# Another order in the HGRN ring, behind it, and at the start of the output stage, of a hybrid decoder layer on one core

## The reference

```python
h = rms_norm(x, norm_g)
aq, ak, av, ag, hq, hf, hi, hg = split(h @ w_in)     # eight groups of 512 columns
o_a = diff_attention(rope(norm(aq)), rope(norm(ak)), av)            # 4 heads, causal
hq = silu(hq);  f = lb + (1 - lb) * sigmoid(hf);  logf = log(f);  hk = 1 - f
# HGRN, 4 heads of 128, in chunks along the tokens, state S (128 x 128 of each head):
b   = cumsum(logf)
att[t, s] = sum_d hq[t, d] * hk[s, d] * exp(b[t, d] - b[s, d])      # s <= t
o_h = att @ hi + (hq * exp(b)) @ S
S   = exp(b_end) * S + (hk * exp(b_end - b)).T @ hi
mix = concat(rms_norm(o_a) * silu(ag), rms_norm(o_h) * silu(hg))
y   = x + mix @ w_out
```

## Time and profile before

| | |
|---|---|
| median of 3 runs | 1703.94 us (1701.72 to 1711.8) |
| the profiled execution | 1702.97 us |
| its span in the trace | 1700.8 us |
| mean granted TensorE clock | 0.975 of full speed |
| PE busy | 1563.5 us (92%) |
| DVE busy | 992.0 us (58%) |
| ACT busy | 774.9 us (46%) |
| POOL busy | 494.2 us (29%) |
| HBM traffic | 100 GB/s over the span |

### The profile page before, as it was taken

One profiled execution on the slowest core, in us unless ns is written; L12 is line 12 of the kernel. 1 busy time (PEld: TensorE's weight loads), 2 busy tenths in 40 slices (PEclk: granted clock), 3 DMA queues, 4 the chain that ended last, 5 costly groups with the idle time before them and its releaser, 6 DMA issues. The chain is left out here.

```text
span 1700.8 us, 24978 instructions
## 1 busy us (share of the span) xinstructions
PE 1563.5 (92%) x9156; PEld 1270.5 (75%) x9156; DVE 992.0 (58%) x2319; ACT 774.9 (46%) x1094; POOL 494.2 (29%) x636
## 2 busy tenths in 40 slices
PE   6799999997999999999999969999999967899998
PEld 5688888885887888878787856767777745677776
DVE  4422222126666677667776749988888865544442
ACT  4233333335455444544455336666667653432320
POOL 1333323233356644665456600000000002222121
PEclk9899999999999999999999989999999987899999
DMA  7533334456001010101001042100000018665651
GB/s 285 192 143 140 123 131 149 149 180 228 26 32 56 32 38 32 56 32 38 32 32 56 7 167 100 51 25 26 14 14 26 14 47 300 229 192 184 217 180 62
DMA packets 79834, 171.59 MB, mean 101 GB/s; under 512 B 9186, under 2 KB 15970, under 8 KB 79714
## 3 DMA queue, kind: packets, MB, share of 16 engines
q1 hardware_dynamic: 79714, 170.00, 29.0%
HBM read 113.35 MB, written 56.62 MB: 100 GB/s over the span
## 5 line engine op out<-in xcount | busy, mean ns | idle before, releaser
L92 PE MATMUL h_banks<-h_w_hi,h_x_hi 128*128 128x512 f32 x1088 | 435.9, 401 | 26.4 <-DVE h_x_lo L651 16.7
L94 PE MATMUL h_banks<-h_w_hi,h_x_lo 128*128 128x512 f32 x1088 | 427.4, 393 | 0.0
L93 PE MATMUL h_banks<-h_w_lo,h_x_hi 128*128 128x512 f32 x1088 | 427.1, 393 | 0.0
L92 PEld LDWEIGHTS h_banks<-h_w_hi,h_x_hi 128*128 128x128 f32 x1088 | 206.9, 190 | 68.9 <-DVE h_x_lo L651 17.2
L94 PEld LDWEIGHTS h_banks<-h_w_hi,h_x_lo 128*128 128x128 f32 x1088 | 206.2, 189 | 44.7
L93 PEld LDWEIGHTS h_banks<-h_w_lo,h_x_hi 128*128 128x128 f32 x1088 | 206.9, 190 | 40.8
L145 POOL TENSOR_TENSOR h_stage_or_levels<-h_stage_or_levels,h_qk_or_hgrn 128x128 f32<-128x128 f32 x192 | 106.9, 557 | 277.3 <-ACT h_stage_or_levels L589 277.3
L1078 ACT ACTIVATE p_scores<-p_scores,p_nmx 128x256 f32<-128x256 f32 (+15 forms) x128 | 153.1, 1196 | 5.8 <-DVE p_nmx L1129 5.5
L1214 PE MATMUL p_ops<-p_V,p_WT 128*128 128x128 f32 x1088 | 146.4, 280 | 8.7 <-ACT p_WT L1087 8.4
L1214 PEld LDWEIGHTS p_ops<-p_V,p_WT 128*128 128x128 f32 x1088 | 132.6, 193 | 15.4 <-ACT p_WT L1087 13.9
L1124 DVE CUSTOM_DVE_ANT_0 p_scores<-p_sps,p_zero 128x512 f32<-128x512 f32 x192 | 122.2, 686 | 15.9 <-PE p_sps L1188 15.7
(11 more groups left out here) (217 smaller groups left out, 2692.2 us busy)
## 6 DMA issues: line engine op xcount, KB each, us to landing
h_stage_or_levels<-in_w_in SPq DMA_DIRECT2D x32, 512.0 KB, 6.5
h_xs_sq_or_tok<-in_xT SPq DMA_DIRECT2D x17, 512.0 KB, 6.1
h_qk_or_hgrn<-in_x SPq DMA_DIRECT2D x17, 512.0 KB, 6.5
tmp_xh_s<-h_x_hi SPq DMA_DIRECT2D x17, 512.0 KB, 3.6
tmp_xl_s<-h_x_lo SPq DMA_DIRECT2D x17, 512.0 KB, 4.7
h_x_hi<-tmp_xh_s SPq DMA_DIRECT2D x17, 512.0 KB, 3.6
h_x_lo<-tmp_xl_s SPq DMA_DIRECT2D x17, 512.0 KB, 4.6
f_xt<-in_x SPq DMA_DIRECT2D x16, 512.0 KB, 3.8
```

What stands on the lines that cost most here:

```text
L92: eng.matmul(out, x_hi[:, k, :], w_hi[:, k, :], start=(k == 0), stop=False)
L93: eng.matmul(out, x_hi[:, k, :], w_lo[:, k, :], start=False, stop=False)
L94: mm = eng.matmul(out, x_lo[:, k, :], w_hi[:, k, :], start=False, stop=(k == KD - 1))
```

## The change

Nothing that is computed changes; instructions stand in another order.

- **PE in a ring step:** query and forget group come whole ahead of `levels` 0; quarters of the gate group, then of the values group, stand between the other pieces; `head_columns` follows `out_rows` 0. The gate group comes ahead of the values, and from tile 1 on they change banks (`bank_of`), with the waits on a bank's reader to match; `gate_input` and `value_input` read the bank that `bank_of` names.
- **DVE:** `forget` stands between the pair sums of heads 1 and 2; in the prologue `pieces(7)` comes behind `forget(0)` (its old place, not shown below, goes).
- **ACT:** a step begins with `inputs_q`; `gate_input` of tile i stands ahead of the exponentials, `value_input` between their halves, and in the last step behind `o_stats`. In the prologue `inputs_f(0)` comes ahead of `pieces(7)`, and values and gate of tile 0 move in between the exponentials.
- **SP:** `again` waits for the values group too; of the last stores, queries, keys, logarithms and gates come ahead of the last tile's output and its state, the values last.
- **Stage 3:** `START` is 13 for 10, and the fixed n of the samples' HGRN go up by 2 (`level_operands` 19 to 21, `decays` 16 to 18, `decay_sums` 14 to 16, `differences` 16 to 18, `leaves` 21 to 23). The first loads are `o_in`, `ng`, `mr`, `ga`, weights, page table; `load_y` loads `mr` ahead of `ga`. DVE's `norm(0)` comes ahead of its wait for `ng`, and `lo_part` between the first `w_rest`; ACT's `hi_part` likewise between the first `w_rounded`.

```diff
+def bank_of(i, g):
+
+    if i > 0 and g >= 2:
+        return 3 - g
+    return g % 2
...
                 else:
+                    sp.wait_ge(s["proj"][6], t - 1)
                     sp.wait_ge(s["proj"][7], t - 1)
...
             store(NP - 2)
-            store(NP - 1)
-
-            sp.wait_ge(s["state"], NP + 1)
-            sp.dma_start(io["s_p"].rearrange("h d v -> d h v"), state[:, :, :]).then_inc(s["tail"], 16)
+
             sp.wait_ge(s["qT"], NT)
             sp.dma_start(io["hq_s"], qT).then_inc(s["tail"], 16)
             sp.wait_ge(s["f_clamped"], NT)
             sp.dma_start(io["hk_s"], kT).then_inc(s["tail"], 16)
             sp.wait_ge(s["log_f"], NT)
             sp.dma_start(io["hl_s"], lfT).then_inc(s["tail"], 16)
+            sp.wait_ge(s["gate"], NT)
+            sp.dma_start(io["hg_s"], gate[:, 0]).then_inc(s["tail"], 16)
+            store(NP - 1)
+            sp.wait_ge(s["state"], NP + 1)
+            sp.dma_start(io["s_p"].rearrange("h d v -> d h v"), state[:, :, :]).then_inc(s["tail"], 16)
             sp.wait_ge(s["v_tok"], NT)
             sp.dma_start(io["hv_s"], v_tok[:, 0]).then_inc(s["tail"], 16)
-            sp.wait_ge(s["gate"], NT)
-            sp.dma_start(io["hg_s"], gate[:, 0]).then_inc(s["tail"], 16)
...
             def step(t, pt, more):
                 i, p = t + 1, 1 - pt
-                gate_input(t, pt)
                 inputs_q(i)
                 inputs_f(i)
+                q_columns(i)
                 act.wait_ge(s["kdT_ps"], t + 1)
                 after(act, s["gain_ps"], t)
                 act.activation(kd_tok, kps.rearrange("p h d -> p (h d)"), ACT.Copy).then_inc(s["kd_tok"], 1)
-                q_columns(i)
                 decays(i)
+                gate_input(i, p)
                 if more:
                     exps(i, 0)
-                value_input(i, p)
                 if more:
+                    value_input(i, p)
                     exps(i, 1)
                     tile_decay(p)
                 o_stats(t)
+                if not more:
+                    value_input(i, p)
...
             act.wait_ge(s["x_lo"], NT)
             inputs_q(0)
+            inputs_f(0)
             pieces(7)
-            inputs_f(0)
             act.wait_ge(s["store_q"][0], 32 * 9)
             act.wait_ge(s["store_q"][1], 32 * 8)
             q_columns(0)
             decays(0)
+            value_input(0, 0)
             exps(0, 0)
-            value_input(0, 0)
+            act.wait_ge(s["store_v"], 16 * NT)
+            act.wait_ge(s["store_g"], 16 * NT)
+            gate_input(0, 0)
             exps(0, 1)
             tile_decay(0)
-            act.wait_ge(s["store_v"], 16 * NT)
-            act.wait_ge(s["store_g"], 16 * NT)
             for t in range(NP):
                 step(t, t % 2, t < NP - 1)
-            gate_input(NP, 0)
...
             forget(0)
+            pieces(7)
             cumulate(0)
...
                 keep_pairs(t, 1)
+                forget(i)
                 keep_pairs(t, 2)
-                forget(i)
                 keep_pairs(t, 3)
...
+            def group(i, p, g, parts=range(PIECES)):
+                k = bank_of(i, g)
+                if 0 in parts:
                     pe.wait_ge(s["x2_load"][p], 32 * (i // 2 + 1))
                     if i == 0 and g < 2:
                         pe.wait_ge(s["qk_norm"], 2 * NT - 2)
-                    after(pe, s[("v_tok", "gate", "q_tok", "s_tok")[g]], i if g < 2 else i + 1)
-                for b in range(PIECES):
-                    if b // 2 in halves:
-                        if i == 0:
-                            pe.wait_ge(s["w_lo"], (4 + g) * PIECES + b + 1)
-                        mm = product_quarter(pe, bank[g % 2], x_hi[p], x_lo[p], w_hi[g], w_lo[g], b)
-                if 1 in halves:
+                    elif g < 2:
+                        before = 2 if bank_of(i - 1, 2) == k else 3
+                        pe.wait_ge(s["v_tok" if before == 2 else "gate"], i)
+                    else:
+                        pe.wait_ge(s[("q_tok", "s_tok")[k]], i + 1)
+                for b in parts:
+                    if i == 0:
+                        pe.wait_ge(s["w_lo"], (4 + g) * PIECES + b + 1)
+                    mm = product_quarter(pe, bank[k], x_hi[p], x_lo[p], w_hi[g], w_lo[g], b)
+                if PIECES - 1 in parts:
                     mm.then_inc(s["proj"][4 + g], 1)
...
             def step(t, pt):
                 i, p = t + 1, 1 - pt
                 group(i, p, 0)
+                group(i, p, 1)
                 levels(t, 0)
-                group(i, p, 1, (0,))
+                group(i, p, 3, (0,))
                 levels(t, 1)
                 out_rows(t, pt, 0)
-                group(i, p, 1, (1,))
+                head_columns(i, t)
+                group(i, p, 3, (1,))
                 levels(t, 2)
                 key_rows(t)
                 out_rows(t, pt, 1)
-                head_columns(i, t)
+                group(i, p, 3, (2,))
                 levels(t, 3)
                 out_rows(t, pt, 2)
+                group(i, p, 3, (3,))
                 group(i, p, 2, (0,))
                 out_rows(t, pt, 3)
                 group(i, p, 2, (1,))
-                group(i, p, 3, (0,))
                 gains(t, pt)
-                group(i, p, 3, (1,))
+                group(i, p, 2, (2, 3))
...
-PERIOD, START, FIRST = 11, 10, 2
+PERIOD, START, FIRST = 11, 13, 2
...
-            load(pages[:, :], io["page_table"], "pages")
-            load_y(0)
+            load_y(0, 0)
             load(ng[:, 0], io["subln_g"].partition_broadcast(P).rearrange("p a b -> p (a b)"), "ng")
+            load_y(0, 1)
             for n in range(4):
                 load_w(n)
+            load(pages[:, :], io["page_table"], "pages")
             load_y(1)
             load_x(0)
             for n in range(4, 8):
...
             squares(0)
+            hi_part(0, 1)
             w_rounded(0)
+            hi_part(0, 0)
             w_rounded(1)
-            hi_part(0, 1)
-            hi_part(0, 0)
...
             dve.memset(eps[:, :], EPS).then_inc(s["eps"], 1)
+            norm(0)
             dve.wait_ge(s["ng"], 16)
             dve.tensor_scalar(ng[:, 1], ng[:, 0], 1.0 - LAM_INIT, None, ALU.mult).then_inc(s["ng_scaled"], 1)
-            norm(0)
+            lo_part(0, 1)
             w_rest(0)
+            lo_part(0, 0)
             w_rest(1)
-            lo_part(0, 1)
-            lo_part(0, 0)
             w_rest(2)
             w_rest(3)
```

More of the change, by code:

```diff
@@ L561, in gate_input @@
                 after(act, s["o_out"], i - 1)
-                act.activation(gate[:, p], bank[1], ACT.Silu, scale=col(i)).then_inc(s["gate"], 1)
+                act.activation(gate[:, p], bank[bank_of(i, 3)], ACT.Silu, scale=col(i)).then_inc(s["gate"], 1)
             def inputs_q(i):
@@ L580, in value_input @@
                 act.wait_ge(s["proj"][6], i + 1)
-                act.activation(v_tok[:, p], bank[0], ACT.Copy, scale=col(i)).then_inc(s["v_tok"], 1)
+                act.activation(v_tok[:, p], bank[bank_of(i, 2)], ACT.Copy, scale=col(i)).then_inc(s["v_tok"], 1)
             def decays(i):
@@ L729, in _ @@
             pieces(6)
-            pieces(7)
             def keep_pairs(t, h):
@@ L840, in _ @@
                 job(g, NP - 1)
-            def group(i, p, g, halves=(0, 1)):
-                if 0 in halves:
+            def group(i, p, g, parts=range(PIECES)):
+                k = bank_of(i, g)
+                if 0 in parts:
                     pe.wait_ge(s["x2_load"][p], 32 * (i // 2 + 1))
@@ L1351, in load, with load_y @@
                 sp.dma_start(dst, src).then_inc(s[done], 16)
-            def load_y(i):
+            def load_y(i, half=None):
                 p, rows = i % 2, P if i < NP else NS
@@ L1360, in load_y @@
                     sp.wait_ge(s["r_store"], 16)
-                sp.dma_start(o_in[0:rows, p], io["o_s"][r, :]).then_inc(s["o_load"][p], 16)
-                if i >= 2:
-                    sp.wait_ge(s["gated"], i - 1)
-                sp.dma_start(ga[0:rows, p], io["ga_s"][r, :]).then_inc(s["ga_load"][p], 16)
-                sp.dma_start(mr[0:rows, p], io["mr_s"][r, :]).then_inc(s["mr_load"][p], 16)
+                if half != 1:
+                    sp.dma_start(o_in[0:rows, p], io["o_s"][r, :]).then_inc(s["o_load"][p], 16)
+                if half != 0:
+                    sp.dma_start(mr[0:rows, p], io["mr_s"][r, :]).then_inc(s["mr_load"][p], 16)
+                    if i >= 2:
+                        sp.wait_ge(s["gated"], i - 1)
+                    sp.dma_start(ga[0:rows, p], io["ga_s"][r, :]).then_inc(s["ga_load"][p], 16)
             def load_x(i):
@@ L1525, in _ @@
                     gates(i + 2)
-                if n == 19:
+                if n == 21:
                     level_operands()
@@ L1598, in _ @@
                     squares(i + 2)
-                if n == 16:
+                if n == 18:
                     decays()
@@ L1764, in _ @@
```

(6 more changed lines are left out.)

## The result

The changed kernel takes 1658.97 us (median of 4 runs, 1657.05 to 1663.87), against 1707.87 (1701.72 to 1714.65) for the kernel before beside it: a ratio of 0.9731, 95% interval 0.9703 to 0.9759, 2.7% faster (48.9 us by the medians; two more sets of runs of it, in the experiments, are 42.3 and 39.8 us below the kernel before beside them). The profiled execution took 1657.05 us (span 1655.3), the one before 1702.97 (span 1700.8).

The account below looks back on a forecast made before the run. A closed chain of TensorE, DVE and POOL, 34.83 us a ring step, was taken as the bound. Gains of 3.6 (prologue), 29.5 (ring), 7.85 (tail) and 2 (stage 3), 42.95 us, from 1702.97 gave 1660.0 us, range 1647 to 1680.

Parts of the forecast that it names:

- The circle: Ring step: the chain from `levels` 0 through `forget`, scan and POOL's products sets the step, 34.83 us falling to 32.89.
- The hold: Ring: `forget`'s SBUF instructions on DVE wait until POOL's `gated` ends, so a step gains 1.94 us and not 2.38.
- the rival: Ring: `forget` and `gated` run side by side, DVE not kept waiting, a step of 32.45 us, 1653 us; chance 0.27.
- TensorE doesn't stop them: Ring: both forecast steps, 32.45 and 32.89 us, stay above the 31.85 us of TensorE's own work.
- a floor: Ring: 34.83 us less 2.98 us of weight-load waits leaves 31.85 us, which no order of the same work goes under.
- What was costed at nothing: Ring: an extra ACT table load and later gate, value and reload work stay covered and add 0 us to the step.
- (a) to (d): Ring: waits around `gate_input`, `value_input`, the forget group's bank and SP's reload of x, each covered, costing nothing.
- ACT's cover: Ring: the gate's Silu and table load end 4.6 us before the differences are ready; past that each us costs every step.
- Ahead of the ring: Prologue: `inputs_f(0)` ahead of the pieces brings the first `levels` 0 forward by 3.6 us, bounds 0 to 3.6.
- Behind the ring: From the last `levels` 0 to stage 2's first load: 36.33 us becomes 28.48, a gain of 7.85 us.
- Stage 3: Stage 3: earlier `norm(0)` and `lo_part` against later sample work, bounds 8 us less to 4 more, taken as 2 us.
- The sum: Whole kernel: gains of 3.6, 29.5, 7.85 and 2 make 42.95 us off 1702.97, giving 1660.0 us; chance 0.47.

Follow-up runs that it names:

- longer hold: The changed kernel with one more POOL product of 128x640 elements between the two of `gated` in steps 1 to 15: 1677.4 us, 0.9843.
- the kernel without the hold: The changed kernel with POOL's `gated(t)` made to wait for `forget(t+2)`, the one it ran beside: 1653.58 us, 0.9702.
- the eight copies: The changed kernel with eight more 128x512 copies on ACT ahead of the first exponentials of each step but the last: 1663.26 us, 0.976.

## Why the prediction was right, point by point

**The circle.** Right but for its last link. 34.83 became 32.85 where 32.89 was forecast, and its marks (`levels` 1 to 3, mask products, scan) came within 0.2 us of the forecast ones. That a microsecond added to `forget` costs a microsecond (longer hold), and that the step shrinks when the hold goes, shows that the chain from L through the mask products and `forget` to `levels` 3 sets the step. From there two ways lead to the next L. The forecast one, by scan and POOL, ends at L+32.70 in the step shown, 0.2 us sooner than forecast. TensorE's own work behind `levels` 3 ends last: L comes 0.07 to 0.23 us behind POOL's end in the 15 steps, where 0.04 to 0.07 is all that lies between them in every step of the kernel before and of the one without the hold. So the match to 0.04 us is two errors of 0.2 that cancel, and that is luck; the 2 us are not.

**The hold.** Right in kind and size: 0.43 became 1.01 us, and taking it away gives 32.48, the rival's 32.45. The held instruction was to end at L+10.49 (10.06 and its own 0.43) and ended at L+10.29; the first step, without `gated`, was forecast at 32.45 and took 32.51. (The prediction takes 2.8 us from the last mask product to the scan in one sum and 2.71 in the other; with 2.71 in both, the step without hold would have been 32.33.) The nearest row, L651, was the right one to price it with, though that instruction reads two SBUF tiles and this one reads one. The Trainium skill ("SBUF — State Buffer", section "Who interferes with whom") names a tensor_scalar in two-port mode as one that is locked out. The trace agrees, 1.01 for 0.43; that this instruction ran in that mode no run here shows. The lock, which the Trainium skill states for one whole instruction, was longer in the run with the added product: 2.13 us, across the end of one POOL product and all of the next.

**TensorE doesn't stop them.** Nearly right, from a floor that was too low. In the changed kernel POOL's first half ends at 734.50 and L is 734.71 with no wait named: TensorE comes last by 0.2 us. 31.85 took out the 47.6 us that the weight loader waited; at the same places TensorE itself waited 34.0, since matmuls went on meanwhile:

```profile
PE h_banks L885 <- DVE h_qk_or_hgrn L741: 18.9, 16, 1.2
PE h_banks L876 <- POOL h_stage_or_levels L150: 15.1, 16, 1.0
```

That leaves 34.83 - 34.0/16 = 32.7 us, as does its busy time in the earlier trace rows (112.68 of 120). Ends of matmuls are modelled, so this is no hard floor either: the changed kernel still has small waits (0.28 and 0.47 in the step shown), and without the hold the 0.47 went and the step fell to 32.48. There the profile has TensorE busy for 120.00 of 120 us, so, as far as modelled ends can tell, little is left for order.

**What was costed at nothing.** The waits (a) to (d) never showed in the step. ACT's cover was 3.99 us (forecast 4.6), but "past it each us is a us of every step" was wrong for the first microsecond, as the eight copies showed.

**Ahead of the ring.** 3.6 was forecast, 6.53 came, of which 4.0 stood before the edit had any effect: the first head columns lay between 411.5 and 413.8 us in the runs of the new ring, and at 415.64 in the one profile of before. What is the edit's is 2.5 us. The end of the last weight piece on ACT, the scan, and POOL's end, before and after:

```profile
422.13 1.06 ACT L460 ACTIVATE h_w_hi<-h_stage_or_levels 128x1024 fp32r<-128x1024 f32 x1 [0.26 <-DMA h_stage_or_levels<-in_w_in]
429.35 1.37 DVE L759 TENSOR_TENSOR_SCAN h_qk_or_hgrn<-h_qk_or_hgrn 128x128 f32<-128x128 f32 x4 [0.70 <-ACT h_qk_or_hgrn L585]
```

```profile
419.03 1.06 ACT L468 ACTIVATE h_w_hi<-h_stage_or_levels 128x1024 fp32r<-128x1024 f32 x1 [0.28 <-DMA h_stage_or_levels<-in_w_in]
422.55 1.37 DVE L768 TENSOR_TENSOR_SCAN h_qk_or_hgrn<-h_qk_or_hgrn 128x128 f32<-128x128 f32 x4 [1.21 <-ACT h_qk_or_hgrn L593]
437.51 1.29 POOL L150 TENSOR_TENSOR h_stage_or_levels<-h_stage_or_levels,h_qk_or_hgrn 128x512 f32<-128x512 f32 x1
```

ACT's chain gave what was forecast: from the piece's end to the scan it is 6.16 us before and 2.46 after, 3.7 less. But the piece, which waits for its load, ends 8.45 us behind the first head columns for 7.55 before, which takes 0.9 back, and L comes 0.34 us behind POOL's end for 0.05. That 0.34 is seen in two of the eleven profiles with the new prologue, both at a low clock (last section); in the other nine POOL sets L, 0.04 to 0.06 us ahead of it, as the forecast held. In the eleven L comes 26.6 to 27.7 us behind the first head columns, 2.4 to 3.4 sooner than in the one profile of before.

What the forecast overlooked is that the new ring puts the forget group ahead of the first `levels` too. With the old prologue TensorE then sets L, 3.07 us behind POOL; of the 5.9 us that the edit won, 3.4 only paid this back. `inputs_f(0)` moved ahead of the pieces cured it, since TensorE then idles 0.87 us and not 9.34 ahead of its second head columns. The forecast, which held that this idle time doesn't count, had the cure for another reason: luck.

**Behind the ring.** Right: 28.20 us for 28.48 forecast, with the norm's store at L+23.26 (forecast 23.3) and the last one at L+24.10 (24.1), and 36.51 when undone.

**Stage 3.** The 2 us came as 2.15, about the middle of bounds that were wide. Its first product came 5.5 us earlier where 4.5 was the most, so more was given back than thought. Waits that stay are there to take it (PE waited 7.13 us for the samples' keys, about the 7.29 of before), but which of them does is not shown.

**The sum.** 42.95 forecast, 45.5 measured in the spans. The ring, the tail and stage 3 account for 0.7 of the difference, the prologue's edit takes 1.1 away, the stretch ahead of it adds 4.0 and stage 2 takes 1.06. Neither of the last two was edited: stage 2 took 393.0 to 400.3 us in these profiles, and the granted clock goes with it. From 15 to 10 us before its end the clock was 0.50, the lower level, in six of the 14 profiles, which took 397.5 to 400.3 us, and 1.00 in the eight others, the kernel before and the changed one among them, which took 393.0 to 397.0. So the medians agree to 1 us partly by luck; the part that rests on the argument is the ring and the tail, 37.9 for 37.35.

## What to carry to other kernels

Write the step of a hand-ordered ring as one closed chain with its length, and price an edit by what it takes out of that chain; busy shares (94% before) say only how far it can go. When an instruction is moved, look at what the other engines do at its new time: a DVE instruction from SBUF to SBUF that lands beside POOL work can lose there over a third of what the move brings (here 0.37 of 0.97 us a step), and one wait on the other engine gave it back. When work moves ahead of a ring's first step, go through the prologue again with the new order, since another engine may set its end (here TensorE, 3.07 us behind POOL).

## What the hardware showed that was not expected

POOL's products in a row were not parted by a waiting DVE instruction: it came inside one and ran only after the following one too (2.13 us for 0.43). The other way round, POOL's first product of a half takes 1.50 us while differences run on DVE and 0.46 when they are done, so an early start there is worth less than it seems.

The granted clock did not follow from the length of a gap alone. In the changed kernel TensorE had no matmul for 2.10 us ahead of 432.21, and over the next 4 us the granted clock was 0.57, near the lower of its two levels (1.2 of 2.4 GHz), and full again behind that. In the kernel without the hold it had none for 2.05 us ahead of 432.17, and the clock stayed at 1.00. Windows of that stretch, columns as in the earlier trace rows, two of the changed kernel and then one of the other:

```profile
432.00:436.00 4.00, 3.79 (x10) 3.01 (x11) 0.00 (x0) 3.95 (x5) 4.00 (x11) 0.57 0.00 0
436.00:440.00 4.00, 4.00 (x22) 3.37 (x21) 0.00 (x0) 3.52 (x4) 4.00 (x6) 1.00 0.00 0
```

```profile
432.00:436.00 4.00, 3.83 (x17) 3.19 (x18) 0.00 (x0) 3.95 (x5) 4.00 (x11) 1.00 0.00 0
```

Of the eleven profiles with this prologue the clock fell there in two (behind 2.10 and 1.90 us) and held in nine (behind as much as 2.10 us, with START 10). What decides it is open.
